# Five edits in a fused decoder step on one core: entry products of 344 columns, a deeper pipeline for the stick scores, keys first in the merged stage, w_out loaded a stage early, one accumulating gather per tile at the end

## The chip, the core and the metric

The kernel runs on one core of one Trainium2 chip. Five engines each work through a list of their own and wait for one another by semaphores: TensorE (PE, with its weight loads as PEld), VectorE (DVE), ScalarE (ACT), GpSimd (POOL) and SyncE (SP), which here only issues DMAs. The metric is device microseconds of one execution. All data are fp32; each fp32 product is two MATMUL instructions in the trace, so eight products of a 1024-long contraction show as x16.

## The reference

One inference step of a one-layer hybrid trunk for a prompt of 1024 tokens and 32 sample tokens (8 sequences of 4), 1056 in all, model width 1024:

```
h = layer_norm(x)
z = h @ w_in                     # 2568 columns, split among four mixers
oa = stick-breaking attention (4 heads x 64); sample rows also see 256 paged past keys
ob = gated spatial mixing    oc = causal pooling    od = gated delta rule
h = layer_norm(ALPHA*h + [oa|ob|oc|od] @ w_out)
h = layer_norm(ALPHA*h + cross_attention(h, memory of 256 tokens))
f = sum over the 2 chosen of 16 experts: gate * (silu(h@wg) * (h@wu)) @ wd
y = layer_norm(ALPHA*h + f)
```

In stick-breaking attention each score block z needs softplus(z), a suffix sum of it over later keys, and exp(z minus that sum). Keys, values, new states and the memory's keys and values are outputs too.

## The kernel before

The tokens lie in 9 tiles: 8 of 128 prompt rows and one of the 32 sample rows. The program is a chain of stages, each a block with one list per engine and a barrier at its end. Within a stage the order on every engine is written out by hand. The stages that the change touches, with their lines:

- **Entry** (`stage_entry`). SP loads x tiles, the gain and bias of the layer norm, and three column groups of w_in: 512 (K and V), 512 (gate values and pooling values) and 8 (beta and decay). DVE normalises a tile (L283 to L299; the first tile waits for two x tiles), PE transposes it (L455), ACT copies the transposes to hT (L437), and PE makes the three products with the tile's transposed tokens as stationary operand (`project`, L471): 8 products of 512 columns, 8 of 512 and 8 of 8. PE waits for all of w_in before its second turn. The sample tile takes the same 24 products, with 32 stationary columns. ACT copies K, V and the next 512 columns out (L411 to L415), DVE the 8 (L380), and K is turned back by PE (L481).
- **Sticks** (`stage_stick_prompt`). 36 steps of one query block against one key block, for the 8 query blocks; the first step of a query block is its diagonal. A step is: scores on PE (L957), add the bias on DVE (L1039), three activations for softplus on ACT (L1009 to L1011), soft_sum on DVE (L1047, on the diagonal also a mask, L1050), running sums on POOL (L943), the suffix products on PE (L967 and, off the diagonal, L971), argument on DVE (L1056), exp on ACT (L1017), on the diagonal mask_weights on DVE (L1061), values on PE (L987). In iteration n PE does scores(n), suffix(n-1), values(n-2), and DVE does argument(n-2), soft_sum(n-1), add_bias(n).
- **Merged stage** (`stage_sample_and_inputs`). The sample rows' attention over paged keys, together with the input norms and decays of the delta rule. PE turns 4 of 8 key sets (L1170), waits for the decays (`decays`, L1178; they need small DVE and ACT results), turns the other 4, and only then computes sums of squares (L1193) and the scores of all heads (L1207: four products at a time, each into its own 32 output partitions). DVE clears qz (L1296), waits for small loads (L1300), and squares (L1306); ACT does softplus of the scores (L1276 to L1278), the exp, and four rounds of inverse norms (L1271, L1272).
- **Delta** (`stage_delta`). SP loads all of the normalised tokens back into h at its start, though they are first read in the next stage.
- **First residual** (`stage_residual`, tag "o"). SP loads w_out in four pieces of 1 MB; ACT rounds each piece to a high part (L2258), DVE makes the low part (L2231), PE runs three-pass products (L2110 to L2112), DVE adds to h (L2211) and normalises. **Memory** (`stage_memory`) then loads the memory tokens (mem) and the halves of xa_wk and xa_wv; PE turns mem (L2326) and multiplies (L2340).
- **Route** (`stage_route`). DVE builds one-hot matrices; products of them (L2772) give each expert slot its token (row_token). **Experts**: `hidden` on DVE (L3106) multiplies the two halves.
- **Combine** (`stage_combine`). POOL gathers each token's two expert rows by indirect DMA into six slots (L3193); DVE adds them into h, each times its gate (L3219, twice a tile), and takes the statistics (L283 to L285); ACT makes the deviation and applies it to the tile (L3250); DVE multiplies by the gain (L3229); POOL adds the bias (L3206); SP stores.

Of the kernel before, what the change touches and what calls it, by code (L numbers as in the profile page):

```python
# [21 lines left out]
P = 128  # L22
# [13 lines left out]
DH = 64  # L36
# [140 lines left out]
def setup(nc, ctx, T, O):  # L177
# [86 lines left out]
    c.gate, c.off = small(2 * TILES), small(2)  # L264
# [37 lines left out]
def stage_entry(c):  # L302
# [26 lines left out]
    x_in = [s(f"e_x{n}") for n in range(3)]  # L329
    h_out = s("e_h")  # L330
    w_in, const_in, ln_in = s("e_w"), s("e_const"), s("e_ln")
    eps_set, stats, rstd_ok, normed = s("e_eps"), s("e_stats"), s("e_rstd"), s("e_normed")
    turned, hT_ok, proj_kv, proj_vx, proj_ba = s("e_turned"), s("e_hT"), s("e_kv"), s("e_vx"), s("e_ba")
    kv_out, vx_out, ba_out, k_turned, kT_ok = s("e_kvo"), s("e_vxo"), s("e_bao"), s("e_kt"), s("e_kTo")
    stored = [s("e_stored0"), s("e_stored1")]
    dve_chain, act_chain, zeroed = s("e_dve"), s("e_act"), s("e_zero")
    w_view = T['w_in'][0].rearrange("(k p) n -> p k n", p=P)

    with nc.Block() as block:
        @block.sync  # L340
        def _(sp):
            for i in range(TILES):
                sp.dma_start(h[0:rows(i), i, :], x_tile(T, i)).then_inc(x_in[min(i // 2, 2)], 16)
                if i == 0:
                    sp.dma_start(g, row_bc(T['ln0_g'])).then_inc(ln_in, 16)
                    sp.dma_start(b, row_bc(T['ln0_b'])).then_inc(ln_in, 16)
                if i == 1:
                    sp.dma_start(wt[:, :, 0:512], w_view[:, :, KA:KA + 512]).then_inc(w_in, 16)
                    sp.dma_start(wt[:, :, 512:1024], w_view[:, :, VB:VB + 512]).then_inc(w_in, 16)
                    sp.dma_start(wt[:, :, 1024:1032], w_view[:, :, BD:BD + 8]).then_inc(w_in, 16)  # L350
# [3 lines left out]
            for i in range(TILES):  # L354
                sp.wait_ge(normed, i + 1)
                sp.dma_start(c.tokens_dram[i * P:i * P + rows(i), :], h[0:rows(i), i, :]).then_inc(h_out, 16)
                sp.wait_ge(kv_out, 2 * i + 2)
# [13 lines left out]
        def _(dve):  # L371
# [6 lines left out]
            def evac_ba(i):  # L378
                dve.wait_ge(proj_ba, i + 1)
                nc.vector.tensor_copy(c.ba[0:rows(i), i, :], ps[4][0:rows(i), 0:8]).then_inc(ba_out, 1)  # L380

            for i in range(TILES):
                dve.wait_ge(x_in[min(i // 2, 2)], 32 if i < 4 else 16 * (TILES - 4))
# [8 lines left out]
                if i >= 2:  # L392
                    evac_ba(i - 2)
            evac_ba(TILES - 2)
            evac_ba(TILES - 1)

        @block.scalar
        def _(act):
# [6 lines left out]
            def evac(i):  # L405
                r = rows(i)
                act.wait_ge(proj_kv, i + 1)
# [3 lines left out]
                nc.scalar.copy(ktok[0:r, i % 2, :], ps[2 + 4 * (i % 2)][0:r, 0:256]).then_inc(kv_out, 1)  # L411
                nc.scalar.copy(vtok[0:r, i, :], ps[2 + 4 * (i % 2)][0:r, 256:512]).then_inc(kv_out, 1)
                act.wait_ge(proj_vx, i + 1)
# [2897 lines left out]
```

## Time and profile before

| what | us |
|---|---|
| median of 3 runs (1684.13 to 1684.91) | 1684.21 |
| the profiled execution | 1684.2 |
| its span, first to last instruction | 1682.4 |

PE is busy for 1386.1 us of the span, DVE 747.3, ACT 448.1, POOL 207.7. The mean granted TensorE clock is 0.908. The stages from barrier to barrier, with PE's busy time and the granted clock (1.00 is 2.4 GHz, 0.50 is 1.2 GHz):

| stage | from, us | to, us | PE busy | clock |
|---|---|---|---|---|
| entry | 0.0 | 174.8 | 152.13 | 1.00 |
| sticks | 364.0 | 500.7 | 113.72 | 0.94 |
| merged stage | 500.7 | 535.4 | 25.08 | 0.85 |
| delta | 535.4 | 702.0 | 141.85 | 0.85 |
| first residual | 702.0 | 827.1 | 108.50 | 0.92 |
| memory | 827.1 | 903.0 | 62.71 | 0.88 |
| route | 1236.0 | 1289.4 | 23.50 | 0.66 |
| experts | 1289.4 | 1606.9 | 289.77 | 0.96 |
| combine | 1606.9 | 1682.4 | 0.00 | 0.50 |

Read it stage by stage: a barrier stands between them, so what an edit is worth is what its own stage ends earlier. A busy PE in the rows has modelled ends: the distance from one start to the next is the pace.

### The profile page before, as it was taken

The numbers are of one execution on the slowest core, as the hardware profiler recorded it, in microseconds if no ns is written. First come the engines' busy times: TensorE is split into PE (matmuls) and PEld (weight loads), VectorE is DVE, ScalarE is ACT, GpSimd is POOL, SyncE is SP. The second block draws the span as 40 slices with busy tenths as digits, with TensorE's granted clock in tenths as the row PEclk, the third lists the DMA queues.
The fourth block names the chain that finished last, engine by engine and source line by source line (L and its number), as shares of the span: only waits on it lengthen the run. The fifth ranks groups of instructions, "written<-read, shape, count | busy, mean of one in ns | idle before, by whom it ended". The sixth has DMA issues, their size and how long they took to land. (4 is left out here: it accounts for less than half of the span.)

```text
span 1682.4 us, 24853 instructions
## 1 busy us (share of the span) xinstructions
PE 1386.1 (82%) x9807; PEld 936.7 (56%) x9808; DVE 747.3 (44%) x1132; ACT 448.1 (27%) x928; POOL 207.7 (12%) x196
## 2 busy tenths in 40 slices
PE   4999899778886997699698998969961998999900
PEld 2554799654444787488446987858821333333300
DVE  3321545237655564576401003346535443444368
ACT  1111424236765332322101214431110111111122
POOL 0000000003332751000000000000000110111056
PEclk9999899879997998599798999989985999999955
DMA  8110111022002100300351115430054495772153
GB/s 316 38 57 30 34 49 51 18 76 57 1 1 93 29 4 4 117 22 1 115 185 38 38 50 194 157 133 1 1 237 192 157 360 211 275 295 99 51 220 139
DMA packets 76946, 174.30 MB, mean 104 GB/s; under 512 B 12932, under 2 KB 40715, under 8 KB 70435
## 3 DMA queue, kind: packets, MB, share of 16 engines
q1 hardware_dynamic: 67387, 137.73, 23.2%
q0 software_dynamic: 5856, 21.24, 3.7%
q10 hardware_dynamic: 3600, 13.90, 2.0%
q8 instruction: 73, 1.20, 0.3%
q14 instruction: 30, 0.25, 0.0%
HBM read 142.27 MB, written 30.66 MB: 103 GB/s over the span
## 5 line engine op out<-in xcount | busy, mean ns | idle before, releaser
L2997 PE MATMUL bank<-arena,hT 128*64 x384 | 173.7, 606 | 11.3 <-DVE hT L3106 4.9
L2998 PE MATMUL bank<-arena,hT 128*64 128x512 f32 x384 | 173.7, 606 | 0.0
L471 PE MATMUL bank<-arena,hT 128*128 128x512 f32 (+3 forms) x432 | 141.1, 481 | 0.0
L2997 PEld LDWEIGHTS bank<-arena,hT 128*64 128x64 f32 x384 | 53.5, 140 | 124.2 <-issue 124.2
L3116 DVE COPY arena<-arena 128x4096 f32 x24 | 55.1, 2295 | 131.3 <-PE bank L2998 119.3
L471 PEld LDWEIGHTS bank<-arena,hT 128*128 128x128 f32 (+1 forms) x432 | 68.5, 184 | 72.8 <-issue 72.8
L2965 POOL DMA_INDIRECT hT<-tokens,row_token x24 | 40.3, 1678 | 440.4 <-PE bank L2982 229.8
L2111 PE MATMUL bank<-hT_rest,f_w_high 128*128 128x352 f32 x288 | 93.7, 326 | 0.0
L3021 PE MATMUL bank<-arena,hT 128*64 x192 | 87.5, 598 | 2.4 <-ACT hT L3061 2.4
L3023 PE MATMUL bank<-arena,hT 128*64 128x512 f32 x192 | 87.5, 598 | 0.0
L1577 PE MATMUL bank<-arena 64*64 64x64 f32 (+1 forms) x1920 | 68.6, 224 | 3.5 <-DVE arena L1950 3.0
L1577 PEld LDWEIGHTS bank<-arena 64*64 64x64 f32 x1920 | 64.2, 136 | 11.0 <-issue 6.5
L2110 PE MATMUL bank<-hT_high,q_w_high 128*128 128x352 f32 x192 | 62.6, 326 | 7.6 <-DVE q_w_low L2401 7.6
L2110 PE MATMUL bank<-o_w_high,o_s_high 128*128 128x512 f32 (+1 forms) x144 | 57.6, 400 | 12.6 <-DVE o_w_low L2231 12.6
L2110 PE MATMUL bank<-w_w_high,w_s_high 128*128 128x512 f32 (+1 forms) x144 | 57.5, 399 | 10.6 <-DVE w_w_low L2231 10.6
L2110 PE MATMUL bank<-f_h_high_a,f_w_high 128*128 128x352 f32 x180 | 59.2, 329 | 6.6 <-DVE f_w_low L668 6.6
L3061 ACT COPY hT<-bank 128x256 f32<-128x256 f32 x24 | 8.9, 373 | 204.6 <-PE bank L3009 202.3
L2112 PE MATMUL bank<-hT_high,q_w_low 128*128 128x352 f32 x192 | 63.3, 329 | 0.0
L2111 PE MATMUL bank<-hT_low,q_w_high 128*128 128x352 f32 x192 | 63.0, 328 | 0.0
L967 PE MATMUL bank<-arena,const 128*128 128x512 f32 x72 | 42.7, 677 | 21.4 <-DVE arena L1050 11.8
L2340 PE MATMUL bank<-arena 128*128 128x512 f32 x128 | 57.2, 609 | 2.0 <-DMA arena<-in_xa_wk_dram 2.0
L2112 PE MATMUL bank<-f_h_high_a,f_w_low 128*128 128x352 f32 x180 | 58.8, 327 | 0.0
(484 smaller groups left out, 2979.3 us busy)
## 6 DMA issues: line engine op xcount, KB each, us to landing
arena<-in_ex_wg_dram SPq DMA_DIRECT2D x16, 1024.0 KB, 7.5
arena<-in_ex_wu_dram SPq DMA_DIRECT2D x16, 1024.0 KB, 10.2
arena<-in_ex_wd_dram SPq DMA_DIRECT2D x16, 1024.0 KB, 12.3
expert_rows<-hT ACTq DMA_DIRECT2D x24, 512.0 KB, 5.2
arena<-in_cache_mem_k_dram SPq DMA_DIRECT2D x8, 1024.0 KB, 4.9
arena<-in_w_in_dram SPq DMA_DIRECT2D x12, 512.0 KB, 3.9
h<-in_x_prompt_dram SPq DMA_DIRECT2D x8, 512.0 KB, 8.9
arena<-in_w_in_dram SPq DMA_DIRECT2D x2, 2048.0 KB, 17.1
```

What stands on the lines that cost most here:

```text
L471: last = nc.tensor.matmul(ps[bank][0:r, 0:n], hT[:, k, i * P:i * P + r], wt[:, k, col:col + n], start=(k == 0), stop=(k == KC - 1))
L967: last = nc.tensor.matmul(ps[4 + n % 2][:, :], K("negsuf"), sp_[:, n % 3].rearrange(flat), start=True, stop=(kb == qb))
L1577: last = nc.tensor.matmul(out(q, hd), stationary(q, hd), moving(q, hd), start=True, stop=True)
L2110: nc.tensor.matmul(out, high, w_high, start=start, stop=False)
L2111: nc.tensor.matmul(out, high, w_low, start=False, stop=False)
L2112: return nc.tensor.matmul(out, low, w_high, start=False, stop=stop)
L2340: last = nc.tensor.matmul(ps[4 + u % 4][:, :], memT[:, k, m * P:(m + 1) * P], w[:, half % 3, k, :], start=(k == 0), stop=(k == KC - 1))
L2997: nc.tensor.matmul(ps[UPB[u % 2]][0:LR, :], xT[:, u % 2, k, 0:LR], gate_up_of[:, bass.ds(slot, 1), :, k, :].rearrange("p a g f -> p (a g) ...
L2998: last = nc.tensor.matmul(ps[UPB[u % 2]][LR:P, :], xT[:, u % 2, k, LR:P], wB_gate_up[:, :, k, :], start=(k == 0), stop=(k == KC - 1))
L3021: nc.tensor.matmul(ps[DNB[q]][0:LR, :], hidT[:, u % 2, f, 0:LR], down_of[:, bass.ds(slot, 1), f, n].rearrange("p a n -> p (a n)"), start=( ...
L3023: last = nc.tensor.matmul(ps[DNB[q]][LR:P, :], hidT[:, u % 2, f, LR:P], wB_down[:, f, n], start=(f == 0), stop=(f == 1))
L3116: nc.vector.tensor_copy(wB[:, 0:2 * EW], c.xw[:, bass.ds(e & 3, 1), 0:2 * EW].rearrange("p a n -> p (a n)")).then_inc(copied_up, 1)
```

## The change

- Entry: the 1032 columns of w_in are taken as three products of 344 columns, each waiting for its own part of w_in; the five PSUM banks 2, 3, 4, 6, 7 are used in a ring; each x tile has its own semaphore; DVE copies the last third out. The sample tile becomes four products at a time (256, 256, 256 and 264 columns), each into its own 32 output partitions of one bank, and DVE copies them out, keys and values too.
- Sticks: PE issues scores(n+1) in iteration n; zb has 4 slots instead of 3; DVE's order is add_bias, soft_sum, mask_weights, argument; ACT does softplus before weights.
- Merged stage: PE turns all keys before anything else needs them, DVE copies even sets and ACT odd ones, qz is cleared on POOL, and the decays, their copies and exps come after the scores.
- Delta loads w_out into h; the first residual reads it there and loads the nine h tiles from DRAM after the last low part is made; when its last product is done SP loads mem and the first half of xa_wk.
- Combine: `hidden` multiplies by the slot's gate (row_gate, made in the route stage by the one-hot products, now 48 columns wide). The first of a token's two rows is gathered with an add into h itself, the second into a buffer of its own; DVE adds that and does the whole normalisation; POOL only issues gathers.

The core of the diff:

```diff
 stage_entry
+    W3 = 344
+    BANKS = (2, 3, 4, 6, 7)
-                for bank, col, n, out_sem, free in ((2 + 4 * (i % 2), 0, 512, proj_kv, kv_out), ...
+                for n in range(3):
+                    if i == 0:
+                        pe.wait_ge(w_in[n], 16 * len(THIRDS[n]))
...
+                        last = nc.tensor.matmul(bank_of(i, n)[:, 0:W3], hT[:, k, t], wt[:, k, n * W3:(n + 1) * W3],
+                                                start=(k == 0), stop=(k == KC - 1))
+            def project_sample():
...
+                for k in range(KC):
+                    for j in range(4):
+                        n = 264 if j == 3 else 256
+                        last = nc.tensor.matmul(bank_of(NT, 0)[j * NS:(j + 1) * NS, 0:n], hT[:, k, SEQ:TOK],
+                                                wt[:, k, j * 256:j * 256 + n], start=(k == 0), stop=(k == KC - 1))
-            pe.wait_ge(w_in, 48)
 stage_stick_prompt
+            scores(0)
             for n in range(N + 2):
-                if n < N:
-                    scores(n)
+                if n + 1 < N:
+                    scores(n + 1)
...
             for n in range(N + 3):
+                if n < N:
+                    add_bias(n)
+                if 1 <= n <= N:
+                    soft_sum(n - 1)
                 if n >= 3 and steps[n - 3][0] == steps[n - 3][1]:
                     mask_weights(n - 3)
                 if 2 <= n <= N + 1:
                     argument(n - 2)
-                if 1 <= n <= N:
-                    soft_sum(n - 1)
-                if n < N:
-                    add_bias(n)
 stage_sample_and_inputs, PE
-            decays()
             for b in range(4, DB):
                 turn(b)
             square_sums(0)
...
             square_sums(1)
+            decays()
             square_sums(2)
+            pe.wait_ge(gd, 6)
 stage_sample_and_inputs, ACT, after inverse_norms(1)
             act.wait_ge(arg_ok, 1)
             nc.scalar.activation(z, z, ACT.Exp).then_inc(exp_ok, 1)
+            act.wait_ge(gd, 6)
+            nc.scalar.activation(c.egc, c.log_decay, ACT.Exp).then_inc(ga, 1)
+            nc.scalar.activation(c.kgf, c.kgf, ACT.Exp).then_inc(ga, 1)
             inverse_norms(2)
 stage_delta and stage_residual
-            sp.dma_start(c.h[:, 0:NT, :], c.tokens_dram[0:SEQ, :]...).then_inc(sx["hin"], 16)
+            load_w_out(c, sp)
...
+            if split:
+                sp.wait_ge(wl_ok, 4)
+                for i in range(TILES):
+                    sp.dma_start(h[0:rows(i), i, :], c.tokens_dram[i * P:i * P + rows(i), :]).then_inc(h_in[i], 16)
+                sp.wait_ge(prod, 2 * TILES)
+                load_memory_first(c, sp)
 stage_route
+                ins = vt.tensor_tensor(x[:, :, 1, :], x[:, :, 1, :],
+                                       c.gate[:, q * TILES:(q + 1) * TILES].unsqueeze(2).to_broadcast([P, TILES, NL]), ALU.mult)
...
+            link(vt.tensor_copy(c.row_gate, ps[3][:, MOE_TILES:2 * MOE_TILES]))
 stage_combine
+                gp.indirect_dma_start(h[0:r, i, :], None, expert_rows, rows_of(i, 0), compute_op=ALU.add).then_inc(added[i], 16)
+                gp.indirect_dma_start(second[0:r, i, :], None, expert_rows, rows_of(i, 1)).then_inc(second_in[i], 16)
...
+                nc.vector.tensor_tensor(h[0:r, i, :], h[0:r, i, :], second[0:r, i, :], ALU.add).then_inc(summed, 1)
...
+                link(nc.vector.scalar_tensor_tensor(x, x, c.mv[0:r, i % 2, 0:1], g[0:r, :], ALU.subtract, ALU.mult))
+                nc.vector.scalar_tensor_tensor(x, x, c.rstd[0:r, i % 2, :], b[0:r, :], ALU.mult, ALU.add).then_inc(normed, 1)
-                nc.gpsimd.tensor_tensor(h[0:r, i, :], h[0:r, i, :], b[0:r, :], ALU.add).then_inc(normed, 1)
```

## Rows read from the trace of the kernel before

**Rows 1.** Timeline of PE in entry: start us, us, line, operands, count [idle before <-releaser].
```profile
23.55 1.97 PE L455 MATMUL bank<-const,h 128*128 128x128 f32 x8 [3.53 <-DMA arena<-in_w_in_dram]
25.32 17.50 PE L471 MATMUL bank<-arena,hT 128*128 128x512 f32 x48
...
43.58 15.58 PE L471 MATMUL bank<-arena,hT 128*128 128x512 f32 x48
...
158.69 14.41 PE L471 MATMUL bank<-arena,hT 128*32 128x512 f32 x48
```
**Rows 2.** DMA issues of entry's start: count, KB each, median us to landing.
```profile
h<-in_x_prompt_dram SPq DMA_DIRECT2D x1, 512.0 KB, 6.7
...
arena<-in_ln_b_dram SPq DMA_DIRECT2D x1, 512.0 KB, 9.3
...
arena<-in_w_in_dram SPq DMA_DIRECT2D x1, 2048.0 KB, 14.7
```
**Rows 3.** Timeline of PE, full clock: 512 columns, and four at a time.
```profile
518.28 3.66 PE L1207 MATMUL bank<-arena 128*32 128x256 f32 x64
...
869.90 27.63 PE L2340 MATMUL bank<-arena 128*128 128x512 f32 x64
```
**Rows 4.** Timeline of PE in the sticks, one step off the diagonal.
```profile
430.37 1.12 PE L967 MATMUL bank<-arena,const 128*128 128x512 f32 x2 [0.95 <-DVE arena L1047]
...
432.92 0.71 PE L957 MATMUL bank<-arena 64*128 64x128 f32 x8
433.74 1.12 PE L967 MATMUL bank<-arena,const 128*128 128x512 f32 x2
```
**Rows 5.** Timeline of DVE in the same steps.
```profile
431.17 1.11 DVE L1061 TENSOR_TENSOR arena<-arena,const 128x512 f32<-128x512 f32 x1
432.39 0.69 DVE L1056 TENSOR_TENSOR arena<-bank,arena 128x512 f32<-128x512 f32 x1
433.00 0.68 DVE L1047 SCALAR_TENSOR_TENSOR arena<-arena 128x512 f32<-128x512 f32 x1
```
**Rows 6.** Timeline of POOL in the sticks, its first and last of 36.
```profile
371.65 0.61 POOL L941 COPY arena<-arena 128x512 f32<-128x512 f32 x1 [196.52 <-DVE arena L1050]
...
496.01 1.26 POOL L943 TENSOR_TENSOR arena<-arena 128x512 f32<-128x512 f32 x1 [2.11 <-issue]
```
**Rows 7.** Timelines of PE and DVE in the merged stage.
```profile
510.60 0.61 PE L1178 MATMUL bank<-small,const 128*128 128x32 f32 x2 [6.55 <-DVE small L1320]
...
504.52 0.20 DVE L1300 TENSOR_TENSOR small<-small,arena 128x36 f32<-128x36 f32 x1 [2.45 <-DMA small<-in_dn_norm_g_dram]
...
522.62 0.52 DVE L1348 TENSOR_SCALAR arena<-bank,arena 128x288 f32<-128x288 f32 x1 [1.99 <-PE bank L1211]
```
**Rows 8.** Timelines of ACT and PE: start of the first residual, and of memory.
```profile
707.30 1.90 ACT L2258 CAST o_w_high<-arena 128x2048 fp32r<-128x2048 f32 x1 [2.87 <-DMA arena<-in_w_out_dram]
...
711.67 0.76 PE L2110 MATMUL bank<-o_w_high,o_s_high 128*128 128x512 f32 x1 [12.63 <-DVE o_w_low L2231]
...
832.08 3.67 PE L2326 MATMUL bank<-const,arena 128*128 128x128 f32 x16 [5.82 <-DMA arena<-in_mem_prompt_dram]
837.71 29.60 PE L2340 MATMUL bank<-arena 128*128 128x512 f32 x64 [1.96 <-DMA arena<-in_xa_wk_dram]
```
**Rows 9.** Timeline of DVE in route: the one-hots times the token numbers.
```profile
1283.25 1.25 DVE L2903 TENSOR_TENSOR arena<-arena 128x432 f32<-128x432 f32 x2
```
**Rows 10.** Timelines of DVE and POOL in combine.
```profile
1614.84 2.69 DVE L3219 SCALAR_TENSOR_TENSOR h<-arena,small,h 128x1024 f32<-128x1024 f32 x2 [11.14 <-DMA arena<-expert_rows,slot]
...
1619.01 2.63 DVE L3219 SCALAR_TENSOR_TENSOR h<-arena,small,h 128x1024 f32<-128x1024 f32 x2
...
1624.21 4.56 DVE L3219 SCALAR_TENSOR_TENSOR h<-arena,small,h 128x1024 f32<-128x1024 f32 x2
...
1624.38 3.31 POOL L3206 TENSOR_TENSOR h<-h,arena 128x1024 f32<-128x1024 f32 x1 [4.80 <-DVE h L3229]
...
1677.72 2.33 POOL L3206 TENSOR_TENSOR h<-h,arena 32x1024 f32<-32x1024 f32 x1 [1.16 <-DVE h L3229]
```

More of the change, by code:

```diff
@@ L1198, in _ @@
                 turn(b)
-            decays()
+            for bank, r, t0, chunks, col in ((5, 3, 0, range(4), 0), (6, 3, 0, range(4, 6), 0), (7, NS, 3, range(4), 0),
+                                             (4, NS, 3, range(4, 6), 0)):
+                for n in chunks:
+                    last = nc.tensor.transpose(ps[bank][0:r, col + (n % 4) * P:col + (n % 4 + 1) * P], c.tail[:, n, t0:t0 + r],
+                                               K("ident"))
+                last.then_inc(st_mm, 1)
             for b in range(4, DB):
@@ L1378, in stage_delta @@
     nc, T, O, K = c.nc, c.T, c.O, c.K
+    c.w_out_in = [c.sem(f"w_out{n}") for n in range(4)]
     PAIRS = NT // 2
@@ L2128, in stage_residual @@
     s = lambda n: c.sem(f"{tag}_{n}")
-    w_in = [s(f"w{n}") for n in range(4)]
+    if split:
+        place_memory(c)
+        c.mem_in, c.half_in = s("mem"), [s(f"half{n}") for n in range(3)]
+    w_in = c.w_out_in if split else [s(f"w{n}") for n in range(4)]
+    raw = h[:, 0:KC, :] if split else w
+    h_in = [s(f"h{n}") for n in range(TILES)] if split else []
     ln_in, prod, added, stats, rstd_ok, normed, turned, hT_ok, low_ok = (
@@ L2149, in _ @@
         def _(sp):
-            for n in range(4):
-                sp.dma_start(piece(w, n), piece(wv, n)).then_inc(w_in[n], 16)
+            if not split:
+                for n in range(4):
+                    sp.dma_start(w_piece(w, n), w_piece(wv, n)).then_inc(w_in[n], 16)
             sp.dma_start(g, row_bc(T[gain][0])).then_inc(ln_in, 16)
@@ L2296, in stage_memory @@
     s = lambda n: c.sem(f"m_{n}")
[L2297 removed]
+    w_in = c.half_in
     c.place(start=c.at["halves"][0] + 4096, qring=4 * KC * P, qhigh=4 * KC * P)
     c.q_in = [s(f"q{n}") for n in range(4)]
[L2300 to L2301 removed]
+    mem_in = c.mem_in
+    turned, mT_ok, prod, out_ok, kturned, kT_ok, stored = (
+        s("turned"), s("mT"), s("prod"), s("out"), s("kturned"), s("kT"), s("stored"))
     with nc.Block() as block:
@@ L2305, in _ @@
         def _(sp):
-            sp.dma_start(mem, T['mem_prompt'][0].rearrange("(m p) n -> p m n", p=P)).then_inc(mem_in, 16)
-            for n in range(4):
+            for n in range(1, 4):
                 if n == 3:
```

368 lines of the change are left out of this document (186 added, 182 removed).

## The prediction, made before the change was run

> **What bounds the kernel now.** I read the stage table first, because barriers part the stages and each edit lives inside one or two of them. Then, for each changed stage, PE's timeline with what ended its idle time, and the timeline of the engine that it waited for. The reader is to see five different limits.
>
> Entry is PE-bound: after a late start, which waits for normalised tiles and for w_in, a prompt tile costs 15.58 us of products and the sample tile, a quarter as tall, still 14.41 [rows 1]. The sticks are close to PE-bound: 36 steps, first to last running sum 371.65 to 496.01 [rows 6], 3.55 us a step, 3.37 off the diagonal (430.37 to 433.74) [rows 4]. The merged stage is a chain: PE stands idle 6.55 us for the decays while half of the keys are not turned yet [rows 7]. The first residual and the memory stage begin with PE waiting for a DMA [rows 8]. Combine has no PE work; DVE is the bound, and it is slowed by POOL: two gated adds of a tile take 2.63 us alone and 4.56 us while POOL adds the bias of another tile for 3.31 us [rows 10].
>
> **Entry, the start.** The first x tile lands 6.7 us after an issue in the first microsecond, the bias of the norm 9.3 us after an issue at about 1.7, so at 11.0 [rows 2]. Before, tile 0 waits for both first tiles. With its own semaphore its statistics run at 7.5 and only the apply waits, till 11.0. Applying takes 3.3 us, tile 1's statistics, deviation and apply 5.4 more: the second turn can begin at 19.9 instead of 23.55 [rows 1]. The part of w_in that is waited for now is a third: a half of it lands 14.7 us after an issue at 2.8 (17.5) [rows 2], the third sooner. Start: **3.6 us**. Covers that could fail: there are five w_in DMAs in place of three ahead of x tile 2 on SP's queue, so that tile lands later; ACT turns to hT(1) only after tile 2's statistics. PE has about 14 us of the first tile's products to cover that; if it is not enough, some microseconds of the 3.6 go.
>
> **Entry, the tiles.** 512 columns at full clock go at 27.63/64 = 0.432 us an instruction [rows 3]. So 32 of them are 13.8 of the 15.58 us, and the 16 instructions with 8 columns take 1.8: 0.11 each, for almost no columns. No row has 344 columns in fp32. If the price goes with the columns it is 0.290 and a tile takes 48 x 0.290 = 13.9; on a straight line from 0.11 at 8 columns it is 0.325, 15.6 a tile, no gain. The 256-column groups of four take 3.66/16 = 0.229 [rows 3], against 0.216 by columns and 0.269 by the line, so I take columns: 1.65 x 8 = **13.2 us**, bounds 0 and 13.6. The new waits (a bank's last copy, on ACT or DVE) each look at a copy made at least a third of a tile earlier and cost nothing.
>
> **Entry, the sample tile.** It becomes 64 instructions in groups of four. The same shape stands in the merged stage: 64 in 3.66 us [rows 3]. 14.41 - 3.7 = 10.7 us less. Its tail grows: K and V used to leave in mid-tile, now DVE copies them (0.4 each) after all products, then SP issues two stores that take 2 us; from the last product to the barrier I make 3.9 us out of 1.7. Net **8.5**. The Trainium skill (TensorE: Matmul & The Clock Gate, Why this matters for your kernels) gives three tiles of 32 columns a speedup of 2.38, not 3; carried to four that would be some 4.5 us for the tile, and the sum 0.8 less. The row shows almost the full four.
>
> Entry together: 3.6 + 13.2 + 8.5 = 25.3.
>
> **Sticks.** Off the diagonal PE's own work is the distance 430.37 to 432.92 plus the scores, eight instructions in about 0.55: 3.10 of the 3.37 us [rows 4]. The rest is a loop: argument (32.39), then soft_sum (33.00) on DVE, whose end at 433.68 releases suffix at 433.74 [rows 4, 5]; the same soft_sum also waits for a softplus that began only after the previous soft_sum and add_bias. With scores and bias one step earlier and DVE's order turned, softplus of a step has ended about 1.9 us before suffix needs it, and ACT's four activations take 2.6 of 3.1 us. So an off-diagonal step becomes PE-bound at 3.12. On the diagonal the step has one suffix product, 2.25; but mask_weights (1.11) [rows 5] now runs behind add_bias and soft_sum, and values waits about 0.65 for it: 2.9. Before, a diagonal step costs about 4.1. A query block of q+1 steps so gains 1.2 + 0.25q; from q = 4 on that is 2.2 + 2.5 + 2.75 + 2.0 = 9.5. The first four blocks run partly at clock 0.50, where PE's work doubles and hides the latency gain; step by step I get 4.6 there. **14 us**, bounds 3 (the loop closes elsewhere) and 17.
>
> **Merged stage.** DVE no longer clears qz but still waits for the small loads until 504.5 before its first key copy [rows 7]. Then: copies 0 and 2, square (1.2) to 507.2, copies 4 and 6 to 508.5, qz to 509.7. PE turns keys until 507.4, does the first sums, and starts the scores at about 509.7 instead of 518.28 [rows 3, 7]: 8.6 us. From scores to end, 12.7 us before (522.62 to 535.3) [rows 7], it becomes longer: the second square (1.25) and the decays' copies (0.9) now lie between the argument and the exp of the decays, for which ACT waits with two rounds of norms behind it, about 2.6. 8.6 - 2.6 = 6.0. PE's gaps are shorter but the stretch is thin, and the clock stood at 0.50 there before; if it falls, the scores take up to 3.7 more and the gain is near 0 to 2. I take **5**, bounds 0 and 8.
>
> **Residual and memory.** The first round of a w_out piece starts at 707.30 after a wait for its DMA of 2.87 [rows 8]; with the piece in h it starts at 704.4, and later pieces come at DVE's 2.3 instead of the DMA's 2.7. PE starts 2.9 earlier: **3.0**. The price is the load of the h tiles behind the last low part, at about 715.5; the first 0.5 MB lands about 3.5 us later, at 719, before the first tile's products end at 720. That cover is 1 us thin; without it DVE has a tile's time (11.8) of slack on PE. In delta a 4 MB load replaces one of equal size. Memory: PE turns mem at 832.08 after 5.82 idle, and multiplies at 837.71 after 1.96 more [rows 8]. With both loads made under the residual's last 10 us, the turns start at 827.3 and the products at 831.5: **6.3**, bounds 4 and 7.5. The second half of xa_wk is issued at the barrier as before, and is needed 14 us after the first.
>
> **Route and experts.** Two more 432-element multiplies at 0.63 [rows 9], and a small copy: **1.7 lost**; the wider one-hot products are bounded by 0 and 1.5. In experts `hidden` gets a second multiply on a DVE that waits for PE; 0.
>
> **Combine.** Per tile DVE will do one add (1.26), the statistics (1.48, from 1614.84 + 2.69 to 1619.01), and two of the 1.3 us forms with their links: 5.33 in all, and POOL no longer reads h, so the uncontended row counts [rows 10]. Nine tiles: 48.0. The first gather landed at 1614.84; now two must, one of them with an add: +2.5. The tail is a store, 2.35 (POOL's last add ends at 1680.05, the span at 1682.4) [rows 10]. 48.0 + 2.5 + 2.4 = 52.9 after 1614.84 in place of 67.6: **14.7**. No row has an accumulating DMA. A plain gather of 0.5 MB costs 1.3 us at the 390 GB/s of that stretch; DVE stays the bound while the adding one costs under 4. The Trainium skill (Collectives: The Full Stack, The bandwidth ceiling) has a reducing transfer run at half rate because it reads two sources: 2.6 us, still under DVE. Bounds of the term: 7 and 17, and below nothing by the first rival.
>
> **The sum.** 25.3 + 14 + 5 + 3.0 + 6.3 - 1.7 + 14.7 = 66.6. The profiled execution took 1684.2 (span 1682.4 and 1.8 around it), the median of the runs 1684.21; so 1684.2 - 66.6 = **1617.6**.
>
> **Rivals.**
> 1. *Slower: the adding gather is serial and expensive.* Place: the nine adding gathers of combine. The rest of the change gives 51.9; combine loses that when it takes 67.6 + 51.9 = 119.5, or 13.3 us a tile, some 12 us for one adding gather, nine times a plain one. At 14.5 a tile the kernel takes about 1695. Against it: a row is one 4 KB piece per token, as in the plain gather. Chance 0.04.
> 2. *The adding gather costs four plain ones*, 5.2 + 1.3 = 6.5 a tile, 58.5 for nine: DMA-bound, combine gains 3.7, total 1628.6. Chance 0.13.
> 3. *The sticks keep their step*: the loop closes over ACT or POOL, whose sum waits for soft_sum too. Gain 3 of 14: 1628.6. Chance 0.13.
> 4. *344 columns cost the line's 0.325*: 13 us less, 1630.8. Chance 0.06.
> 5. *The change doesn't do what it says*: four products into 32 partitions each run one after another in entry. 64 x 0.22 = 14 us, gain 10.4 less: 1628. The merged stage speaks against it. Chance 0.05.
>
> **How the numbers follow.** My forecast has 0.59, with its own range 1609 to 1627: the thin terms are the sticks and combine (4 each), the start of entry, the clock in the merged stage (3 each). To hold 8 in 10 the range takes in rivals 2 to 5 singly: 1605 to 1634. A measurement of this kernel can tell about 0.2%, 3.4 us. Faster by more than that in all cases but the first rival: 0.95; within it 0.01; slower 0.04.
>
> **What would show it.** Entry ending at about 149.5 with 13.9 us a tile and 3.7 for the sample; suffix starts 3.12 apart; the scores of the merged stage 9 us after its start, at clock 1.00; PE waiting for no DMA at the residual's and memory's start; in combine DVE at 5.3 us a tile without waiting for the gathers. The prediction is wrong if x tile 2 starves entry, if DVE in combine waits for DMA, or if clock 0.50 appears where it was 1.00.

## The result, and the profile after

The changed kernel takes **1609.68 us** (median of 4 runs, 1609.42 to 1610.8), before 1684.17 in the same runs: a ratio of 0.9559, 95% interval 0.9542 to 0.9575, so 74.5 us less. The forecast was 1617.6, its range 1605 to 1634. The profiled execution took 1610.8, its span is 1608.8, 73.6 less than the 1682.4 of before.

The table of stages comes first again, because barriers part them. These are the busy times by stretch of the changed kernel: from and to, length, busy time and instruction count of PE, PE's weight load, DVE, ACT and POOL, granted clock, share of the DMA engines, GB/s.

```profile
0.00:150.00 150.00, 128.74 (x538) 87.41 (x539) 49.39 (x87) 25.12 (x78) 0.20 (x4) 1.00 0.36 124
150.00:309.00 159.00, 140.81 (x870) 140.27 (x870) 76.21 (x87) 54.37 (x77) 0.31 (x1) 0.94 0.15 39
309.00:336.30 27.30, 24.61 (x266) 20.26 (x266) 9.20 (x24) 8.64 (x27) 0.00 (x0) 0.81 0.15 55
336.30:454.60 118.30, 109.94 (x704) 57.02 (x704) 84.16 (x136) 88.62 (x145) 43.27 (x36) 0.95 0.13 37
454.60:482.70 28.10, 22.68 (x344) 15.70 (x344) 17.52 (x47) 19.60 (x46) 7.67 (x8) 0.94 0.03 5
482.70:649.00 166.30, 140.53 (x2992) 118.28 (x2992) 89.72 (x248) 51.31 (x146) 67.00 (x95) 0.86 0.11 35
649.00:772.00 123.00, 109.41 (x504) 86.96 (x504) 82.11 (x103) 29.89 (x50) 0.00 (x0) 0.94 0.18 68
772.00:841.50 69.50, 62.88 (x160) 29.95 (x160) 5.54 (x8) 4.40 (x8) 0.00 (x0) 0.92 0.46 155
...
1051.60:1176.70 125.10, 109.53 (x504) 87.10 (x504) 72.31 (x85) 30.28 (x50) 0.00 (x0) 0.93 0.13 45
1176.70:1231.60 54.90, 22.67 (x137) 11.23 (x137) 29.23 (x80) 2.94 (x6) 0.02 (x1) 0.66 0.63 251
...
1547.40:1608.80 61.40, 0.00 (x0) 0.00 (x0) 45.84 (x54) 5.74 (x19) 26.76 (x18) 0.51 0.77 229
```

Set against the same stages of before, the 73.6 us come from the following. (Four bounds of before are read more closely here than in the table of the stages ahead: merged stage to 535.5, memory to 902.7, route from 1235.9 to 1290.1, where POOL issues the first gather of the experts.)

| stage | before, us | after, us | gained | forecast |
|---|---|---|---|---|
| entry | 174.8 | 150.0 | 24.8 | 25.3 |
| features (untouched) | 159.9 | 159.0 | 0.9 | 0 |
| gate and pool (untouched) | 29.3 | 27.3 | 2.0 | 0 |
| sticks | 136.75 | 118.3 | 18.45 | 14 |
| merged stage | 34.75 | 28.1 | 6.65 | 5 |
| first residual | 125.1 | 123.0 | 2.1 | 3.0 |
| memory | 75.6 | 69.5 | 6.1 | 6.3 |
| second residual (untouched) | 123.4 | 125.1 | -1.7 | 0 |
| route | 54.2 | 54.9 | -0.7 | -1.7 |
| combine | 75.5 | 61.4 | 14.1 | 14.7 |
| delta, queries, cross, experts | 693.1 | 692.2 | 0.9 | 0 |

All stages but one lie within 2.0 us of what was forecast. The sticks miss by more, 4.45 of the 7 us that the forecast is short. Three stages that no edit touches move by up to 2 us, in both directions.

**Entry.** Timeline of PE in the changed kernel (start us, us, line, operands, count, idle time before and what ended it), against [rows 1]:

```profile
20.65 1.97 PE L480 MATMUL bank<-const,h 128*128 128x128 f32 x8 [3.42 <-DVE h L299]
22.41 15.94 PE L498 MATMUL bank<-arena,hT 128*128 128x344 f32 x48
...
39.07 14.04 PE L498 MATMUL bank<-arena,hT 128*128 128x344 f32 x48
...
143.04 3.77 PE L508 MATMUL bank<-arena,hT 128*32 128x256 f32 x64
```

The products begin at 22.41 in place of 25.32. A tile takes 14.04 in place of 15.58, which is 0.293 us an instruction of 344 columns; the sample tile takes 3.77 in place of 14.41.

**Sticks.** Timeline of PE, two steps off the diagonal and the step on the diagonal that opens the next query block, against [rows 4]:

```profile
383.88 1.12 PE L1004 MATMUL bank<-arena,const 128*128 128x512 f32 x2
384.84 1.02 PE L1008 MATMUL bank<-arena,const 128*128 128x512 f32 x2
385.79 0.66 PE L1024 MATMUL bank<-arena 128*64 128x128 f32 x8
386.38 0.71 PE L994 MATMUL bank<-arena 64*128 64x128 f32 x8
387.02 1.12 PE L1004 MATMUL bank<-arena,const 128*128 128x512 f32 x2
...
390.17 1.13 PE L1004 MATMUL bank<-arena,const 128*128 128x512 f32 x2
391.23 0.66 PE L1024 MATMUL bank<-arena 128*64 128x128 f32 x8
391.81 0.71 PE L994 MATMUL bank<-arena 64*128 64x128 f32 x8
392.46 1.13 PE L1004 MATMUL bank<-arena,const 128*128 128x512 f32 x2
```

From one suffix product (L1004) to the next it is 3.14 us (383.88 to 387.02) off the diagonal and 2.29 on it (390.17 to 392.46), and no row has an idle time: PE is the bound now.

**Merged stage.** PE's timeline, against [rows 7] and [rows 3]: the scores (L1245) start 8.5 us behind the stage's start (17.5 before), and PE's longest wait comes behind them.

```profile
463.09 3.66 PE L1245 MATMUL bank<-arena 128*32 128x256 f32 x64
...
472.67 3.22 PE L1224 MATMUL bank<-arena,const 128*128 128x352 f32 x6 [2.60 <-DVE arena L1384]
```

**Combine.** Timeline of DVE, against [rows 10]: two waits for gathers, and then tile follows tile without a gap, 5.18 us each (1567.68 to 1572.86).

```profile
1558.78 1.23 DVE L3279 TENSOR_TENSOR h<-h,arena 128x1024 f32<-128x1024 f32 x1 [14.64 <-DMA arena<-expert_rows,slot]
...
1562.47 1.22 DVE L3279 TENSOR_TENSOR h<-h,arena 128x1024 f32<-128x1024 f32 x1 [0.90 <-DMA arena<-expert_rows,slot]
...
1567.68 1.22 DVE L3279 TENSOR_TENSOR h<-h,arena 128x1024 f32<-128x1024 f32 x1
...
1572.86 1.22 DVE L3279 TENSOR_TENSOR h<-h,arena 128x1024 f32<-128x1024 f32 x1
```

### The profile page after: what moved, and what is told of

Read it like the earlier page. It is cut to its first block and busy times, and to the rows that moved or that the text cites. A ratio compares the mean times of both kernels' runs of the same rounds, so it can differ in the third digit from the quotient of the medians.

```text
span 1608.8 us, 24942 instructions
## 1 busy us (share of the span) xinstructions
PE 1353.9 (84%) x9823; PEld 942.6 (59%) x9824; DVE 735.0 (46%) x1154; ACT 425.5 (26%) x897; POOL 189.1 (12%) x188
## 5 line engine op out<-in xcount | busy, mean ns | idle before, releaser
L3071 PEld LDWEIGHTS bank<-arena,hT 128*64 128x64 f32 x384 | 53.3, 140 | 123.6 <-issue 123.6
L3191 DVE COPY arena<-arena 128x4096 f32 x24 | 55.1, 2295 | 130.3 <-PE bank L3072 118.3
L498 PE MATMUL bank<-arena,hT 128*128 128x344 f32 x384 | 114.4, 458 | 0.0
L498 PEld LDWEIGHTS bank<-arena,hT 128*128 128x128 f32 x384 | 73.5, 193 | 37.3 <-issue 1.4
L2145 PE MATMUL bank<-w_w_high,w_s_high 128*128 128x512 f32 (+1 forms) x144 | 58.2, 404 | 10.8 <-DVE w_w_low L2303 10.8
L2283 DVE SCALAR_TENSOR_TENSOR h<-h,bank 128x512 f32<-128x512 f32 (+1 forms) x36 | 24.6, 683 | 74.9 <-PE bank L2147 72.6
## 6 DMA issues: line engine op xcount, KB each, us to landing
arena<-in_ex_wd_dram SPq DMA_DIRECT2D x16, 1024.0 KB, 13.2
```

The source lines that it names most:

```text
L498: last = nc.tensor.matmul(bank_of(i, n)[:, 0:W3], hT[:, k, t], wt[:, k, n * W3:(n + 1) * W3], start=(k == 0), stop=(k == KC - 1))
L2145: nc.tensor.matmul(out, high, w_high, start=start, stop=False)
L3071: nc.tensor.matmul(ps[UPB[u % 2]][0:LR, :], xT[:, u % 2, k, 0:LR], gate_up_of[:, bass.ds(slot, 1), :, k, :].rearrange("p a g f -> p (a g) ...
L3191: nc.vector.tensor_copy(wB[:, 0:2 * EW], c.xw[:, bass.ds(e & 3, 1), 0:2 * EW].rearrange("p a n -> p (a n)")).then_inc(copied_up, 1)
```

## The experiments

Twelve kernels ran, each beside the kernel before, whose medians lay between 1683.85 and 1684.40. The runs of one kernel scatter by 1 to 7 us (those of st_orders2 by 10, 1677.0 to 1687.2), so a total alone tells little below 2 us or so; for small effects the stages' own lengths are read, from one profiled execution of each kernel.

### Each part undone

Five kernels are the changed one with the stage functions of one part put back as they were.

```
u_entry:   stage_entry as before
u_sticks:  stage_stick_prompt as before
u_merged:  stage_sample_and_inputs as before
u_wout:    stage_delta, stage_residual, stage_memory as before
u_combine: stage_route, stage_experts, stage_combine as before
```

> The changed kernel with the entry stage of before (512 + 512 + 8 columns, w_in waited for as a whole, sample tile as one more tile). Theory (the gains of the stages add, because barriers part them): entry's 24.8 us come back, 1609.7 + 24.8 = 1634.5, and every later stage keeps its own time to within 2 us. That rest I ascribe to the moment at which the granted clock goes from 0.50 to 1.00 behind a stage's start: the gate stage, which nothing in the change touches, took 29.3 us before and 27.3 after, with the rise about 11 us behind its start before and 7.5 after. By this theory the gate stage here comes out anywhere between 27 and 30 us, in step with its rise, while its instructions stay the same. Rival (entry's new layout of loads speeds gate itself up): the gate stage goes back to 29.3 with the rise at any place.

> The changed kernel with the stick stage of before. Theory (additive): the stage's 18.5 us come back, 1628.2; first to last running sum 124.4 us again in place of 104.5. Rival (part of the 18.5 us came from an earlier rise of the clock at its start, not from the order): 1625 or less, with the first to the last running sum under 122.

> The changed kernel with the merged stage (the sample's sticks and the delta inputs) of before. Theory (additive): 6.7 us come back, 1616.4, the scores starting 17.5 us behind the stage's start in place of 8.5. Rival (the clock): the stage of before stood at clock 0.50 for part of its first half; if that does not recur, it costs only 3 to 4 us more than the new one, 1613.

> The changed kernel with delta, the residuals and memory of before: w_out is loaded at the residual's start, memory's loads at memory's. Theory: the first residual gives back 2.1 to 3, memory 6.0, together 8.1 to 9, so 1618 to 1619; the first product of the residual 9.6 us behind its start (6.6 in the changed kernel). Rival (the loads only moved DMA time to another stage, which pays for it): under 1614.

> The changed kernel with route, experts and combine of before (gates applied in combine, 18 plain gathers, the norm shared by DVE, ACT and POOL). Theory (additive): combine gives back 14.1, route gains 0.7, experts lose about 1: 1609.7 + 14.4 = 1624.1. Rival (combine's gain rests on its place behind faster stages, not on itself): some other number; within 2 us of 1609.7 would say that the new combine is worth nothing.

| kernel | median, us | ratio to before | lost against 1609.68 | its stages, undone and changed, us |
|---|---|---|---|---|
| u_entry | 1636.12 | 0.971 (0.9685 to 0.9735) | 26.4 | entry 174.6, 150.0 |
| u_sticks | 1627.29 | 0.9662 (0.9639 to 0.9686) | 17.6 | sticks 136.2, 118.3 |
| u_merged | 1617.3 | 0.9602 (0.9583 to 0.9622) | 7.6 | merged 34.4, 28.1 |
| u_wout | 1617.83 | 0.9605 (0.9583 to 0.9626) | 8.2 | residual and memory 200.4, 192.5 |
| u_combine | 1625.45 | 0.9655 (0.9638 to 0.9672) | 15.8 | combine 75.1, 61.4 |

The five losses add up to 75.6 us, and the whole change brought 74.5: the parts add. The rivals of four of these runs fall. The sticks' gain is hardly the clock's: the old order takes 136.2 us in the new surroundings too, and though the changed stage stood at clock 0.50 for 10.8 us where that of before stood for 16.7, the same stage takes 118.9 in u_combine, where it stood there for 14.1. That is 0.6 us for 3.3, so about 1 of the 18.45 us is the clock's by this estimate. The merged stage of before stays at clock 0.50 for as long as it did (10.2 us) and costs 6.3 us. No other stage pays for the earlier loads: delta takes 166.1 us without them and 166.3 with them. Of the 15.8 us of u_combine the stage itself is 13.7; route is 0.7 shorter, and experts is 2.6 longer (319.0 us from SP's first issue, 316.4 in the changed kernel), which was not looked into.

The gate stage speaks to what is left, and to the rival of u_entry. Its code is the same in all kernels. Read in windows of 1 us, it stood at clock 0.50 for 11.9 us before and took 29.3; 11.6 and 29.2 in u_entry; 10.8 and 28.5 in st_scores, a run of the next part; 8.7 and 27.9 in u_sticks; 7.4 and 27.3 in the changed kernel. u_entry by itself doesn't tell my theory from its rival, since length and rise went back together. The others do: st_scores and u_sticks have the changed kernel's code up to the end of this stage, and it still takes 1.2 and 0.6 us longer in them, in step with the rise. The windows of before and of the changed kernel show the two ends.

```profile
334.70:345.00 10.30, 8.50 (x64) 6.42 (x65) 3.64 (x10) 0.70 (x2) 0.00 (x0) 0.50 0.41 142
345.00:355.00 10.00, 10.00 (x120) 8.61 (x121) 3.40 (x8) 4.18 (x14) 0.00 (x0) 0.92 0.01 2
```

```profile
309.00:319.00 10.00, 8.88 (x85) 6.96 (x87) 4.01 (x11) 1.37 (x4) 0.00 (x0) 0.63 0.41 147
319.00:329.00 10.00, 10.00 (x132) 8.54 (x129) 3.89 (x10) 4.55 (x14) 0.00 (x0) 1.00 0.01 2
```

The second residual does the same the other way round: 10.2 us at clock 0.50 and 123.4 to 123.6 us long before and in ten of the other kernels, 13.6 and 125.0 to 125.1 in the changed kernel, in u_entry and, with the old code of the residuals, in u_wout. So a microsecond more at the lower clock costs about half a microsecond, and the length of a stage can move though neither it nor anything ahead of it was edited: by 1.2 us in the gate stage of st_scores, by 1.6 in the second residual of cb_plain. That the clock is what does it is read from this going together in all fourteen kernels; no run set the clock by itself, and what sets the moment of its rise stays open. It is not all of the scatter either: entry, with the changed kernel's code and at clock 1.00 throughout, takes 148.1 us in u_wout and 150.0 in the changed kernel, the longest of the twelve kernels that have it.

### The sticks: lead or order

The change does two things there, it issues the scores a step earlier and turns the orders of ACT and DVE. Two kernels have one of them.

```
 st_scores (scores ahead, orders of before)
 DVE:   add_bias, soft_sum, mask, argument  ->  mask, argument, soft_sum, add_bias
 ACT:   softplus, weights                   ->  weights, softplus

 st_orders2 (new orders, scores in their own step, mask first on DVE)
-            scores(0)
             for n in range(N + 2):
-                if n + 1 < N:
-                    scores(n + 1)
+                if n < N:
+                    scores(n)
```

> The changed kernel, with the scores a step further ahead on PE as in it, but with the old orders on ACT (weights ahead of softplus) and DVE (mask, argument, soft_sum, add_bias). Theory (the loop is closed on DVE: soft_sum stands behind argument, add_bias last): scores that are ready earlier do not help, the step off the diagonal stays at 3.3 to 3.4 us and the stage gains at most 4 of its 18.5 us: 1624 to 1628. Rival (the lead of the scores is what counts): step 3.15, 1610 to 1613.

> The changed kernel with the new order on ACT and DVE, save that the mask of the weights stands first on DVE, and with the scores of a step only issued in that step, as before. Theory (the order is what counts): add_bias now stands ahead of soft_sum and must wait for scores that PE issues behind the last step's values; PE needs soft_sum of the last step right behind them, and between lie add_bias 0.69 + soft_sum 0.68 and the hand-overs, so the step becomes longer than 3.15, 3.4 to 4.2 us, and the stage loses 8 to 35 us: order and lead are only worth something together. 1618 to 1645. Rival (the order alone gives the gain): 1610 to 1612.

**st_scores** takes 1629.51 us (ratio 0.9677, 0.966 to 0.9694), its stick stage 136.2: the lead alone brings nothing at all, and the total lies above my 1624 to 1628. Timeline of DVE in it, one step of 3.37 us:

```profile
429.38 0.69 DVE L1094 TENSOR_TENSOR arena<-bank,arena 128x512 f32<-128x512 f32 x1 [1.48 <-PE bank L1008]
429.99 0.68 DVE L1085 SCALAR_TENSOR_TENSOR arena<-arena 128x512 f32<-128x512 f32 x1
430.59 0.68 DVE L1077 TENSOR_TENSOR arena<-bank,arena 128x512 f32<-128x512 f32 x1
432.75 0.69 DVE L1094 TENSOR_TENSOR arena<-bank,arena 128x512 f32<-128x512 f32 x1 [1.48 <-PE bank L1008]
```

The argument waits for the sums of its step (L1008), soft_sum stands behind it, and PE's next suffix, which needs nothing but soft_sum, starts at 430.73, 0.06 behind its end. That is the loop of before: sums 1.98, argument and soft_sum 1.3, hand-overs.

**st_orders2** takes 1684.47 us (0.9992, 0.9975 to 1.001). The order alone eats all that the other stages gained: the stage is 192.5 us long in the profiled execution (1687.23 us, the slowest of its ten), 56 more than with everything old; by the medians it is some 3 us less. I had expected 8 to 35 us of loss and a step of 4.2 at most. It is 4.63 at full clock, as the rows and their releasers show (timeline of PE):

```profile
467.43 0.71 PE L994 MATMUL bank<-arena 64*128 64x128 f32 x8
469.56 1.13 PE L1004 MATMUL bank<-arena,const 128*128 128x512 f32 x2 [1.42 <-DVE arena L1084]
470.52 1.02 PE L1008 MATMUL bank<-arena,const 128*128 128x512 f32 x2
471.47 0.66 PE L1024 MATMUL bank<-arena 128*64 128x128 f32 x8
```

PE's scores (467.43) release add_bias at 468.21, soft_sum follows at 468.82, and its end releases the suffix at 469.56. So the loop runs through PE's whole step (sums 1.91, values 0.59, scores 0.78) and then through two operations of DVE (1.35): 4.63. My expectation had counted DVE's two and left PE's own queue out of the loop. Lead and order are each worthless or harmful, and together worth 18 us.

### Combine: the price of the adding gather

```
 cb_plain
-  gp.indirect_dma_start(h[0:r, i, :], ..., rows_of(i, 0), compute_op=ALU.add)
+  gp.indirect_dma_start(first[0:r, i, :], ..., rows_of(i, 0))
   ...
+  link(nc.vector.tensor_tensor(h[0:r, i, :], h[0:r, i, :], first[0:r, i, :], ALU.add))

 cb_both
   for i in range(TILES):  gather 0 of tile i, adding into h
-  (in the same loop) gather 1 of tile i, plain, into second; DVE adds it
+  for i in range(TILES):
+      gp.wait_ge(added[i], 16)
+      gather 1 of tile i, adding into h
```

> The changed kernel in which both gathers of combine are plain, into buffers of their own, and DVE adds both to h. Theory (the DVE bound goes up by one add of 1.25 us a tile; adding rows cost the DMA engines about twice a plain row, which was hidden): a tile takes 6.4 us on DVE, 9 of them 58; the first add starts 1.5 to 2.5 us earlier than in the changed kernel (11.4 us behind the stage's start), combine 69 to 71 us, total 1618 to 1620. The share of the software queue goes from 53 % of 61.4 us, 521 engine-us, to about 400. Rival (adding costs what a plain gather costs): the same 520 engine-us, the first add no earlier, 1621.

> The changed kernel in which the second gather of combine adds into h too: nine adding gathers, then nine more, each behind the first of its tile; DVE has no add left (3.95 us a tile). Theory (an adding gather costs the DMA engines about 38 engine-us, twice the 19.6 of a plain one, and now the engines are the bound): 18 of them 43 us, the loads of gain and bias 2.6, the stores that fall among them up to 9, from about 5 us behind the stage's start; combine 63 to 67 us in place of 61.4, total 1611 to 1616. The software queue takes about 650 engine-us (521 in the changed kernel, 353 with plain gathers). Rival (the 521 came from crowding, an adding gather by itself costs a plain one): DVE stays the bound, combine 57 to 58, total 1606.

**cb_plain** takes 1618.35 us (0.9608, 0.9589 to 0.9627), combine 68.5. DVE is the bound with 6.43 us a tile (1566.27 to 1572.70 between two first adds). Timeline of DVE, its first two adds:

```profile
1555.39 1.23 DVE L3279 TENSOR_TENSOR h<-h,arena 128x1024 f32<-128x1024 f32 x1 [10.56 <-DMA arena<-expert_rows,slot]
1557.14 1.23 DVE L3281 TENSOR_TENSOR h<-h,arena 128x1024 f32<-128x1024 f32 x1 [0.53 <-DMA arena<-expert_rows,slot]
```

The first add comes 7.3 us behind the stage's start, 4.1 earlier than in the changed kernel, where I had said 1.5 to 2.5; but it needs one gather only. The second, which needs both as the changed kernel's first add does, comes at 9.1 in place of 11.4, so 2.3 us is what the adding costs there, with 0.65 of it in POOL's longer issue (1.59 in place of 0.94). Combine is a little shorter than my 69 to 71. **cb_both** takes 1619.34 us (0.9616, 0.96 to 0.9632), combine 69.6. The DMA section of each (throughput over 40 equal slices, and the queue of the gathers) follows, first of the changed kernel, then of cb_plain, each over its combine stage, then of cb_both, over the 74 us from 1546 to 1620:

```profile
GB/s 67 379 117 184 211 323 270 251 326 224 342 254 272 310 227 371 334 259 318 358 291 275 363 296 264 368 358 347 83 0 128 214 0 5 342 0 0 248 93 85
...
q0 software_dynamic: 2400, 8.65, 53.0%
```

```profile
GB/s 129 287 246 382 382 418 420 420 418 399 411 418 416 420 418 311 306 67 129 177 0 0 227 79 0 0 306 0 0 24 282 0 5 36 270 0 0 146 160 76
...
q0 software_dynamic: 2400, 8.65, 32.2%
```

```profile
GB/s 270 13 263 188 184 210 210 213 213 204 213 213 210 213 213 206 210 210 213 210 213 210 208 232 279 261 279 270 334 286 137 164 69 215 27 257 0 283 71 0
...
q0 software_dynamic: 2400, 8.65, 59.1%
```

The packets and bytes are the same in all three. Plain gathers run at 418 to 420 GB/s, adding ones at 210 to 213. In engine time: 0.322 of 68.5 us of 16 engines is 353 us for 18 plain gathers (I had expected 400); 0.591 of 74 us is 700 for 18 adding ones (650 expected); in the changed kernel 0.530 of 61.4 us is 521, less the nine plain ones 345 for nine adding ones. Two of the 18 are of 32 rows and move a quarter, so the 18 count as 16.5 of 128 rows: 21.4 us of engine time for a plain one, 42.4 and 41.8 for an adding one. So an adding gather costs twice a plain one, 2.6 us of all 16 engines in place of 1.3. The Trainium skill (Collectives: The Full Stack, The bandwidth ceiling) says of the reducing transfers of a ring collective that they run at half the rate, since they read two sources where a copy reads one. By that rule, the traces agree.

cb_both failed my 63 to 67 us, and the theory that the DMA engines bound the whole stage: its first statistics start at 1579.77, 30.8 us behind the stage's start, because all nine first gathers went ahead of the first second one, and from there DVE goes at 3.92 us a tile with one short wait (0.97). First a DMA-bound stretch, then a DVE-bound one, one behind the other, in place of both at once. The order of its gathers is my edit's own, so it says nothing of 18 adding gathers issued in pairs.

### Two attempts to get more

```
 cb_ln:      SP waits for the first adding gather, then loads combine's gain and bias
 mg_decays:  ACT takes inverse_norms(2) ahead of the decays' wait and two exp
 best:       both
```

> The changed kernel in which combine's loads of gain and bias (0.5 MB each) are issued behind the landing of the first adding gather in place of at the stage's start. Theory (the first add, 11.4 us behind the start, waits for DMA engines that these loads share): the first add comes 2 to 2.6 us earlier, DVE keeps its 5.18 us a tile, combine 59 to 59.5, total 1607.3. Rival (the gathers' own latency sets the start): the first add at 11 us or more, total 1609.7; or DVE then waits for the second pair and for gain and bias, with the same total.

> The changed kernel in which ACT, in the merged stage, makes the two exp of the decays behind the third round of norms in place of ahead of it. Theory (ACT stands idle 2.02 us for the decays' copies with the norms ready behind them, and the end of the stage is ACT's chain of norms): the idle time goes, the stage takes 26.0 to 26.5 us in place of 28.1, total 1607.7. Rival (the end is set by the sticks' own chain, weights, turns, values, output): stage 27.5 to 28.1, total 1609.5.

> The changed kernel with the two last edits together (gain and bias of combine loaded late, decays' exp behind the norms). If both theories hold 1605.2; by the rivals 1609.5.

They took 1609.25 (0.9559, 0.9542 to 0.9577), 1608.32 (0.9552, 0.9537 to 0.9568) and 1609.94 us (0.9567, 0.9552 to 0.9582); none can be told from the changed kernel's 0.9559.

**cb_ln** did what it was to do and gained nothing: the first add comes 9.1 us behind the start in place of 11.4, and the time is given back at once. Timeline of DVE:

```profile
1552.01 1.23 DVE L3280 TENSOR_TENSOR h<-h,arena 128x1024 f32<-128x1024 f32 x1 [12.34 <-DMA arena<-expert_rows,slot]
...
1557.89 1.23 DVE L3280 TENSOR_TENSOR h<-h,arena 128x1024 f32<-128x1024 f32 x1 [3.09 <-DMA arena<-expert_rows,slot]
...
1562.22 1.28 DVE L3291 SCALAR_TENSOR_TENSOR h<-h,small,arena 128x1024 f32<-128x1024 f32 x1 [1.53 <-DMA arena<-in_ln_b_dram]
```

The second pair now waits 3.09 us where it waited 0.90, while the two loads go over the same DMA engines, and the bias is late by 1.53. Combine is 63.0 us long, 1.6 more than in the changed kernel, which the total doesn't show. This is the rival's second half, which I had put at no change. In **mg_decays** ACT's 2.02 us for the decays is gone, and a wait of 0.94 for the third group's sums of squares is there in its place, which PE gets late from DVE (its wait of 2.60 for L1384 in the rows above): the stage takes 26.8 us in place of 28.1. The clock is not what shortens it: in cb_plain the stage stood at 1.00 throughout as well and took 28.1. That 1.3 us is below what the totals can show, and with the other edit the stage took 27.5.

## Why the prediction was right, point by point

The mechanisms hold term by term, and the one mis-sized term is the sticks. That the sum is not further off is in part cancelling, as the points show. The forecast is short by 7.0 us of the span: 4.45 in the sticks, 1.65 in the merged stage, 1.0 in route and 2.1 in stages that have no term, less 2.2 by which entry, the residual, memory and combine fell short.

**Entry, the start (3.6; measured 2.9).** The first tile's statistics ran at 8.49, not 7.5, and the apply at 11.8, not 11.0; the chain behind them was as worked out. None of the named covers failed: x tile 2 was late (DVE waited 6.13 us for it) and PE never saw it. The first tile took 15.94 us for 48 instructions that take 14.04 elsewhere; so it had before (17.50 for 15.58), and the excess of 1.9 is no part of the gain. In other kernels with the same code it took 14.65 to 15.95.

**Entry, the tiles (13.2; measured 8 x 1.54 = 12.3).** The choice between 0.290 and 0.325 an instruction went by the 256-column row, and 344 columns cost 0.293: the fixed share of the 8-column products was no fixed share of wider ones. Rival 4 falls. **The sample tile (8.5 net):** 10.6 less on PE as said; the tail from the last product's end (146.8) to the barrier (150.0) is 3.2, where I had worked out 3.9. Rival 5 falls: 64 in 3.77 us. The Trainium skill (TensorE: Matmul & The Clock Gate, Why this matters for your kernels) has a speedup of 2.38 for three such tiles, which carried to four is an estimate of 4.5 us. The rows differ and decide: the full four.

**Sticks (14; measured 18.45), the one term mis-sized.** The step off the diagonal was right: PE-bound at 3.12, measured 3.14. The step on the diagonal was put at 2.9, made of 2.25 on PE and 0.65 of waiting for mask_weights; it is 2.29 where the rows stand, and 2.45 as a mean (a query block of five steps takes 15.05 from 374.25 to 389.30, less 4 x 3.15). Eight diagonals at 0.45 are 3.6 of the 4.45 us. The failing step is "mask_weights (1.11) [rows 5]": I carried its duration over, and it now takes 0.68, so values no longer waits for it where the rows stand. Timeline of DVE and then of POOL in the changed kernel:

```profile
393.81 0.68 DVE L1099 TENSOR_TENSOR arena<-arena,const 128x512 f32<-128x512 f32 x1
```

```profile
394.02 1.60 POOL L980 TENSOR_TENSOR arena<-arena 128x512 f32<-128x512 f32 x1 [1.01 <-POOL arena L980]
```

Before, POOL's sum had started first (430.45, 1.28 us) and DVE's mask ran beside it from 431.17 for 1.11. Now the mask starts first, takes 0.68, and POOL's sum takes 1.60 where others take 1.28. In both pairs the one that comes second pays, 0.43 or 0.32. The Trainium skill (SBUF — State Buffer, Who interferes with whom) says that a DVE instruction with two SBUF inputs contends with a GpSimd instruction that reads SBUF, and that issue order decides who blocks. Both pairs of rows agree with it, and the delay is less than the overlap (0.43 of 0.56 us, 0.32 of 0.47). I had read [rows 5] as the cost of the operation, and it was the cost of its place. A further 1.2 us is in the first four blocks, for which I gave 4.6 and which gained 7.6 (371.65 to 409.55 before, 343.94 to 374.25 after) with 1.8 of the difference on the diagonals. Another 1.0 is in the last block: my sum has 2.0 for it where its own 1.2 + 0.25q gives 2.95, and it gives no reason. And 1.4 go the other way, because the stage now ends 6.2 us behind its last running sum and not 4.7. Rival 3 falls.

**Merged stage (5; measured 6.65).** By its working 8.6 less 2.6: the scores came 9.0 us earlier, ACT lost 2.02 on the decays, and from the scores' end to the barrier it is 15.4 in place of 13.0. The deduction of 1 us for the clock was not needed; it stood at 1.00 until well behind the scores. My working had the clock only as a risk, and it is part of the gain: before, the clock fell to 0.50 while PE stood idle for 6.55 us [rows 7], and the second half of the turns and the sums of squares took 3.67 and 2.79 us. They take 1.97 and 2.01 now, which is some 2.5 of the 9.0 us.

**First residual and memory (3.0 and 6.3; measured 2.1 and 6.1).** The first product came 6.6 us behind the start in place of 9.6, as said. The thin cover held: h's first tile landed at 665.4, DVE waited 2.18 us for it, and PE is busy without a gap from 660 to 685. The missing 0.9 us is of the size that the clock moves: with the same code the stage took 121.8 to 123.4 us in the other kernels.

**Route (-1.7; measured -0.7).** The term was right, and the clock hid it. From DVE's first operation behind the activations to the stage's end it is 35.65 us before (1254.45 to 1290.1) and 37.2 after (1194.38 to 1231.58), 1.55 more; the products ahead of that take 15.90 us in place of 16.77, at clock 0.91 in place of 0.86. In cb_plain, with the same code, they take 16.77 again and the stage 0.8 to 0.9 us more than in the changed kernel. The wider one-hot products cost nothing (4.08 and 4.05).

**Combine (14.7; measured 14.1).** DVE at 5.18 us a tile, not 5.33; the start 3.5 us later, not 2.5 (first add 11.4 us behind the start, 7.9 before). The step that was too small is "+2.5" for two gathers in place of one, "one of them with an add": it is 3.5, and by cb_plain 2.3 of it is the adding. There is also one wait of 0.90 for the second pair, for which I had nothing. The adding gather costs 2.6 us of all engines, under the 4 from which DMA would decide. Rivals 1 and 2 fall. Rival 2's own sum is half a microsecond off (67.6 less 58.5, 2.5 and 2.4 is 4.2, not 3.7), and nothing hangs on it. What I had not seen is how little slack is left: the DMA share of the stage is 0.77 and close to full until the last gather, and cb_ln's start gave back what it had gained.

**What the sum left out.** The untouched stages: +0.9, +2.0 and -1.7, the last two in step with where the clock rises in them, and +0.9 in the four of the table's last line. They are no part of the change, and nothing in the trace of before said which way they would go.

## What to carry to other kernels

In a loop over several engines, write the cycle down with every queue that it passes, PE's own included: an order and a lead that are worthless or ruinous singly (0 and -56 us) can be worth 18 us together. A duration read beside another engine's work is the price of that place, so when a change moves the instruction, take the uncontended row and ask who comes second now. A gather that adds cost double in DMA time here; it pays as long as the compute engine stays the bound, and a load put off from a full DMA phase into the same phase gained nothing.

## What the runs showed of the hardware

- An accumulating gather moves 210 to 213 GB/s where the plain one moves 418 to 420, and its issue keeps POOL for about 1.55 us in place of 0.94.
- fp32 products of 344 columns cost 0.293 us an instruction at full clock, near the rate of 512 columns (0.432) and of 256 in groups of four side by side (0.229 a group); only products of 8 columns (0.11) have a floor that shows.
- Where a DVE and a POOL operation that both read two tiles of SBUF met, the one that started later was delayed: 1.11 us for 0.68 on DVE, or 1.60 for 1.28 on POOL.
- Stages with the same instructions differed by up to 2 us between kernels, the gate stage and the second residual in step with how long the clock stayed at 0.50 in them, entry at clock 1.00 throughout.
